# Second block's attentions on one core: a bank for the value products, row halves in turns, earlier compressed turns, squares paired by GpSimd

## The reference, cut to what matters

```python
h = rmsnorm(x, mix_norm[l])
proj = h @ w_in[l]                       # queries, keys, values, gates of both attentions
# sparse attention: 8 heads in 2 groups, head size 64
k_cmp, v_cmp = nsa_compress(...)         # 15 compressed keys/values of the 256 tokens
o_a = nsa_attention(q, k_cmp, v_cmp, k_slc, v_slc, k_win, v_win, gates_a, rel_table)
# linear attention with decay: 4 heads, key size 128, value size 256, chunks of 64 tokens
o_b = gla_attention(q_b, k_b, v_b, log_a)
o_b = rmsnorm(o_b, gla_out_norm)         # over the 256 values of each head: mean of squares
o_b = o_b.reshape(B, S, 1024) * silu(r_b)
y = gm0 * (o_a @ w_branch_nsa) + gm1 * (o_b @ w_branch_gla)
x = x + y @ w_out
```

## Time and profile before

| | |
|---|---|
| median of 3 runs | 2722.19 us |
| lowest, highest | 2721.77, 2728.16 us |
| profiled execution | 2728.3 us, its span 2726.5 us |
| TensorE busy | 2664.9 us, 98% |
| VectorE, ScalarE, GpSimd busy | 1065.1, 1295.2, 1768.0 us (39%, 48%, 65%) |
| mean granted clock of TensorE | 0.991 |

### The profile page before, as it was taken

The page is one execution under the profiler, slowest core; times in us unless marked ns, Lnnn a source line. Parts: engine busy times, 40 slices in busy tenths (PEclk is TensorE's granted clock), DMA queues, the critical chain, the costliest instruction groups (busy, mean ns, idle before and its releaser), DMA issues.

```text
span 2726.5 us, 43454 instructions
## 1 busy us (share of the span) xinstructions
PE 2664.9 (98%) x17423; PEld 2298.5 (84%) x17423; DVE 1065.1 (39%) x2194; ACT 1295.2 (48%) x1851; POOL 1768.0 (65%) x1446
## 2 busy tenths in 40 slices
PE   7999999999999999999999999999999999999998
PEld 5767688778888677988878999999899899989887
DVE  4153564441211545253454322553423414354441
ACT  4445622342222448445545545555545535554553
POOL 2502345334445244868969988559998997757996
PEclk9999999999999999999999999999999999999999
DMA  7564365323223332555635567435555557534554
GB/s 235 147 217 140 124 206 165 109 84 102 93 93 99 68 112 63 155 171 176 205 130 179 191 172 221 125 109 184 187 185 184 186 185 192 171 109 155 185 185 147
DMA packets 397910, 418.81 MB, mean 154 GB/s; under 512 B 80975, under 2 KB 361671, under 8 KB 397492
## 3 DMA queue, kind: packets, MB, share of 16 engines
q1 hardware_dynamic: 397748, 416.52, 49.8%
HBM read 415.42 MB, written 3.16 MB: 154 GB/s over the span
## 4 chain that ended last, share of the span: by engine, by line
PE 91%; DVE 3%; ACT 3%; POOL 1%; issue 1%; DMA 1%; SPq 0%; DVEq 0%; ACTq 0%; POOLq 0%
PE ps L1003 21%; PE ps L987 18%; PE ps L971 14%; PE ps L1655 12%; PE ps L1014 10%; PE ps L1663 6%; PE ps L1031 2%; PE ps L1530 2%; PE ps L1556 2%; POOL ring_r L2066 1%; PE ps L1539 1%; PE ps L1562 1%; ACT arena L2371 1%; PE ps L1786 1%; DMA ring<-in_w_ada 1%
## 5 line engine op out<-in xcount | busy, mean ns | idle before, releaser
L2066 POOL TENSOR_TENSOR ring_r<-ring,ring_hi 128x512 fp32r<-128x512 f32 (+1 forms) x1440 | 1765.5, 1263 | 941.4 <-ACT ring_hi L2120 916.7
L2120 ACT ACTIVATE ring_hi<-ring 128x2048 fp32r<-128x2048 f32 x312 | 596.8, 1914 | 247.0 <-DMA ring<-in_ffn_w_down 104.4
L1003 PE MATMUL ps<-hT_r,ring_hi 128*128 128x256 f32 (+1 forms) x2816 | 467.0, 324 | 5.2 <-issue 2.3
L1003 PEld LDWEIGHTS ps<-hT_r,ring_hi 128*128 128x128 f32 x2816 | 410.1, 191 | 55.3 <-issue 15.1
L1655 PE MATMUL ps<-hT_r,ring_hi 128*128 128x512 f32 x1408 | 340.6, 393 | 0.0
L1655 PEld LDWEIGHTS ps<-hT_r,ring_hi 128*128 128x128 f32 x1408 | 259.6, 189 | 53.5 <-issue 3.3
L987 PE MATMUL ps<-arena_r,ring_hi 128*128 128x256 f32 (+1 forms) x1712 | 291.0, 316 | 1.9 <-DVE arena_r L3429 1.9
L987 PEld LDWEIGHTS ps<-arena_r,ring_hi 128*128 128x128 f32 x1712 | 250.0, 190 | 22.8 <-DVE arena_r L3429 2.3
L1014 PE MATMUL ps<-hT_r,ring_r 128*128 128x256 f32 (+1 forms) x1408 | 237.1, 321 | 0.0
L1014 PEld LDWEIGHTS ps<-hT_r,ring_r 128*128 128x128 f32 x1408 | 207.2, 190 | 19.6
L1663 PEld LDWEIGHTS ps<-hT_r,ring_r 128*128 128x128 f32 x1440 | 184.5, 191 | 6.9
(11 more groups left out here) (401 smaller groups left out, 3363.9 us busy)
## 6 DMA issues: line engine op xcount, KB each, us to landing
ring<-in_w_in SPq DMA_DIRECT2D x74, 1024.0 KB
ring<-in_w SPq DMA_DIRECT2D x64, 1024.0 KB
ring<-in_ffn_w_up SPq DMA_DIRECT2D x44, 1024.0 KB
ring<-in_ffn_w_gate SPq DMA_DIRECT2D x44, 1024.0 KB
ring<-in_ffn_w_down SPq DMA_DIRECT2D x44, 1024.0 KB
ring<-in_w_ada SPq DMA_DIRECT2D x28, 1024.0 KB
arena<-in_w_ada SPq DMA_DIRECT2D x18, 1024.0 KB, 7.8
ring<-in_w_in SPq DMA_DIRECT2D x48, 256.0 KB
```

Of the source, the lines that this page charges most:

```text
L1003: mm = pe.matmul(o, w[0], a[x], start=j == 0 and x == 0, stop=False, skip_group_check=True)
L2066: ins = pool.tensor_tensor(k.ring_lo[s][:, part], k.ring[s][:, part], k.ring_hi[s][:, part], ALU.subtract)
L2120: act.activation(k.ring_hi[s][:, :], k.ring[s][:, :], ACT.Copy).then_inc(k.hi_ready[s], 1)
```

## The change

Five things change, all in the second block's attentions.

1. Bank 7 (`VALUES`) is set aside for the value products of the sparse attention; the others rotate over seven banks meanwhile. TensorE waits before each pair of units until bank 7 has been read.
2. The compressed scores take turns between the row halves product by product, in two banks.
3. The state products of chunks 0 and 1 take turns in the same way, in four banks taken at once; chunk 2 follows.
4. The compressed probabilities are turned in step 1, and the wait for their copy stays in step 2.
5. GpSimd adds the two squares of each head in place (`squares_paired`, four instructions of 128 x 256), in its program before the low part of panel 62 (`PAIRED`). TensorE then waits for `ob_paired` and makes four products with ones instead of eight.

```diff
-    def rotate(self, n):
-        self.bank, self.rotating = 0, n
+    def rotate(self, n, first=0):
+        self.bank, self.rotating = first % n, n
+PAIRED = 62
+VALUES = BANKS - 1
             def sparse_attention(compressed, keys_in):
+                T.rotate(VALUES, T.bank)
                 pe.wait_ge(*k.moved(compressed))
-                for a in range(2):
-                    b = bank()
-                    at = slice(HD * a, HD * a + HD)
-                    for q in range(2):
-                        for c in range(4):
-                            o = (q * 4 + c) * NCMP
+                bs = [bank() for _ in range(2)]
+                for q in range(2):
+                    for c in range(4):
+                        o = (q * 4 + c) * NCMP
+                        for a, b in enumerate(bs):
+                            at = slice(HD * a, HD * a + HD)
                             mm = products(ps[:, b, o:o + NCMP], [(qa[at, c, q * P:q * P + P], kcmp[at, :])])
-                    mm.then_inc(k.bank_done[b], 1)
+                            if (q, c) == (1, 3):
+                                mm.then_inc(k.bank_done[b], 1)
...
-                    if u == 2:
+                    if u == 1:
                         pe.wait_ge(S["cmp_prob"], T.next("cmp_prob"))
...
-                        pe.wait_ge(*k.moved(T.last()))
+                        compressed_turned = T.last()
+                    if u == 2:
+                        pe.wait_ge(*k.moved(compressed_turned))
...
                         if q == 0:
-                            pv = bank()
+                            pv, n = T.again(VALUES)
+                            pe.wait_ge(k.bank_read[pv], n - 1)
...
+                T.rotate(BANKS, T.bank)
             def linear_attention(k_turned):
...
-                for n in range(NCH - 1):
-                    rows = slice(CHUNK * (n % 2), CHUNK * (n % 2) + CHUNK)
-                    for hp in range(2):
-                        b = bank()
-                        for j in range(2):
-                            h = 2 * hp + j
+                for chunks in ((0, 1), (2,)):
+                    bs = {(n, hp): bank() for n in chunks for hp in range(2)}
+                    for h in range(GH):
+                        for n in chunks:
+                            rows, b, j = slice(CHUNK * (n % 2), CHUNK * (n % 2) + CHUNK), bs[n, h // 2], h % 2
...
-                pe.wait_ge(S["ob_squared"], T.next("ob_squared", KD))
+                pe.wait_ge(S["ob_paired"], T.next("ob_paired", GH))
...
-                        mm = products(ps[:, b, j * SEQ:j * SEQ + SEQ], [(ones, sq[:, 2 * h + v, :]) for v in range(2)])
+                        mm = products(ps[:, b, j * SEQ:j * SEQ + SEQ], [(ones, sq[:, 2 * (2 * hp + j), :])])
...
+            def squares_paired():
+
+                sq = area(SQO, KD, SEQ)
+                for h in range(GH):
+                    pool.wait_ge(S["ob_squared"], T.next("ob_squared", 2))
+                    pool.tensor_tensor(sq[:, 2 * h, :], sq[:, 2 * h, :], sq[:, 2 * h + 1, :], ALU.add).then_inc(S["ob_paired"], 1)
+
             for l in range(LAYERS):
                 for j in range(PANELS_2):
+                    if j == PAIRED:
+                        squares_paired()
```

More of the change, by code:

```diff
@@ L365, in __init__ @@
             "cmp_max", "cmp_exp", "cmp_prob", "nsa_max", "nsa_exp", "nsa_prob", "oa_rounded",
-            "oa_split", "rb_ready", "gate0_ready", "ob_squared", "ob_ready", "ob_rounded", "ob_split", "merged_plain",
+            "oa_split", "rb_ready", "gate0_ready", "ob_squared", "ob_paired", "ob_ready", "ob_rounded", "ob_split", "merged_plain",
             "merged_rounded")}
@@ L1959, in linear_attention @@
                 pe.wait_ge(*k.moved(k_turned))
-                for n in range(NCH - 1):
-                    rows = slice(CHUNK * (n % 2), CHUNK * (n % 2) + CHUNK)
-                    for hp in range(2):
-                        b = bank()
-                        for j in range(2):
-                            h = 2 * hp + j
+                for chunks in ((0, 1), (2,)):
[3 more added lines that the diff above has]
+                            rows, b, j = slice(CHUNK * (n % 2), CHUNK * (n % 2) + CHUNK), bs[n, h // 2], h % 2
                             mm = products(ps[:, b, j * DV:j * DV + DV],
                                           [(kst[rows, n // 2, h, :], vb[rows, n // 2, h * DV:h * DV + DV])])
-                        mm.then_inc(k.bank_done[b], 1)
+                            if j == 1:
+                                mm.then_inc(k.bank_done[b], 1)
                 states = T.last()
@@ L2783, in sparse_attention @@
                     if u >= 2 and u % 2 == 0:
-                        attended = skip(1)
+                        attended = T.again(VALUES)
                     if u == HEADS:
@@ L3843, in sparse_attention @@
                     if u >= 2 and u % 2 == 0:
-                        out_of[(u - 2) // 2] = T.take()
+                        out_of[(u - 2) // 2] = T.again(VALUES)
                     if u == HEADS + 1:
```

2 lines of the change are left out of this document (1 added, 1 removed).

## The result

The change makes the kernel slower, by 10.1 us between the medians: 2732.12 us median of six runs (2731.11 to 2733.21) against 2721.98 for the kernel before, six runs beside them; estimated ratio 1.0031, 95% interval 1.0021 to 1.0040. That is 10 us more, where 2.4 us less were forecast and the range ended at 2729. The profiled execution of the changed kernel took 2731.1 us, its span is 2729.3 us. The profiled one of before had already lost 6.6 us when the sparse attention of layer 0 began (1710.35 against 1703.74), so lengths of stretches are compared, not the two spans.

The account below looks back on a forecast made before the run. TensorE, busy 98% of the span, bounds the kernel. Gains of 4.5 and 3.9 us (layers 0, 1) against +3.0 a layer from the pairing give -2.4: 2722.2 to 2719.8 us; 8 in 10 range 2712 to 2729.

Parts of the forecast that it names:

- Compressed scores in turns: Sparse attention's 40 small load and product pairs on TensorE: 3.8 to 2.4 us, 1.4 us less a layer, bounds 0 and 1.4.
- Rival 3: Taking turns does nothing for 15-column products: +2.8 us on the forecast, 2722.6; chance 0.09.
- State products: Twelve 64-row products, 24 loads in 3.54 us: taking turns saves 0.1 us, bounds 0 and 0.25.
- Compressed turns earlier: Turns moved from step 2 to step 1 of the sparse attention: net 0.9 us less a layer.
- Value bank: Two waits a layer for VectorE's copy of the value bank go: 1.3 us less; in layer 1 only, 0.6 more.
- Step 8: Turns waiting for VectorE's four scalings (5.25 us) beside GpSimd's low parts: 0.8 us less, bounds 0 and 0.8.
- Ones products: Squares paired by GpSimd save TensorE four products with ones: 1.6 us less a layer.
- Stand in 62: TensorE stands 2.5 us in panel 62 for its low part, queued on GpSimd behind the adds.
- Its low clock: A 2.5 us stand may bring the low clock: no cost after panel 62, 1.8 us after 66.
- the second stand: TensorE waits 2.1 us before panel 66 for GpSimd's late low part, bounds 0 and 3.1.
- Rival 4: Slower: GpSimd's string from adds to 66 is longer beside VectorE's work, and the low clock comes: 2729.4 us; chance 0.12.
- the shared path: GpSimd's SBUF path is shared with VectorE at two SBUF inputs; GpSimd's instructions then take 2.28 instead of 1.28 us.

Follow-up runs that it names:

- stops after each panel: Changed kernel, but GpSimd waits after each of panels 62 to 67 until its own subtractions of that panel are complete; 2722.46 us (before: 2721.47).
- after 62: Changed kernel, but GpSimd waits once, after panel 62, until its own subtractions of that panel are complete; 2720.34 us (before: 2726.44).
- after the first subtraction: Changed kernel, but GpSimd waits once, inside panel 62, after the first of its four subtractions; 2730.54 us.
- the stop after 63: Changed kernel, but GpSimd waits once, after panel 63, until its own subtractions of that panel are complete; 2717.97 us (before: 2726.44).

## Why the prediction was wrong, point by point

- **Compressed scores in turns:** 1.36 us less a layer (3.86 to 2.50), 1.4 forecast. Rival 3 is out.
- **State products:** the 24 loads in 3.32 instead of 3.54 us: 0.2, near the upper bound, forecast 0.1. (The 1.3 us named beside it isn't half of the serial 4.9 us but 4.9 - 3.54.)
- **Compressed turns earlier:** as read. Step 1's turns (1719.04, 1719.48) are followed by products without a gap, and the wait in step 2 is gone: 0.9.
- **Value bank:** the waits went, 1.3 us. In layer 1 the state products waited for it (below): 0.73 us, forecast 0.6.
- **Step 8:** the four scalings take 3.17 us instead of 5.25 once GpSimd's second panel is moved away. With and without the pairing the way to 62 differs by 0.95 us, 0.8 forecast.
- Together 4.7 and 4.0 us, against 4.5 and 3.9. Layer 1 took 1.5 us less on top, as the low clock after the small products didn't come: the 32 products behind them take 4.10 instead of 5.58 us. I had let that gain cancel against a loss.
- **Ones products:** 1.73 us, forecast 1.6.
- **Stand in 62:** 2.37 us, forecast 2.5.
- **Its low clock:** I wrote that it "would cost nothing", since GpSimd would set when 66 begins. It cost 1.43 us in layer 0 and 1.38 in layer 1 (16 products in 3.51 and 3.46 us), as 66 no longer waited for GpSimd. It wasn't certain to come: with the pairing alone the same 2.37 us stop was followed by 16 products in 2.17 us.
- **The step that failed is the second stand.** The sum had VectorE lose nothing to GpSimd and GpSimd 1 us for each of VectorE's long passes, as in the 13.03 us of the earlier trace rows. That price was taken from strings that were 0.6 us old when VectorE asked. The trace of before had the other case too: the 4.26 us of VectorE's line 3022 at 1402.89, eight us into a string, which the prediction doesn't name. In the string that the change makes, 15.2 us old, VectorE loses 9 us (10.72 against 1.77), GpSimd nothing (20 subtractions in 24.86 us). So the stand came one panel earlier (65, for VectorE's reads of PSUM), was 5.0 us long instead of 2.1, and brought the low clock, 2.4 us. With VectorE let in, the stand before 66 that I forecast is there in some form, against 2.1 and bounds of 0 and 3.1: 2.8 to 3.2 us where no low clock followed the stop in 62 (stops after each panel, after 62, after the first subtraction), 0.2 to 0.6 or none where it did.
- **Rival 4** had the right sign and nearly the size (2729.4) with the wrong mechanism: no more slow instructions of GpSimd, but none, and VectorE slow in their place. It got 0.12, since I looked only for what would make GpSimd later. I had also said "the 2.28 us row agrees" of the shared path, and read it in one direction only.

The row for the wait of layer 1's state products on the value bank, loads in the timeline (before 0.17 us idle, now 0.90):

```profile
2435.82 3.32 PEld L973 LDWEIGHTS ps<-arena 64*128 64x128 f32 x24 [0.90 <-issue]
```

## What to carry to other kernels

Work given to an idle engine is priced by what is queued behind it: here 3.4 us of additions (1.22 + 3 x 0.73) at the right place bring 1.7 us a layer, and two panels earlier they cost some 9 (10.1 us above the kernel before with them, 8.7 below it without, over two layers). When a move turns an in-order engine's loose work into one long string, look at who shares a port with it: take every pass of the other engine that reads or writes SBUF beside that string, and price it both ways, by one instruction and by the whole rest of the string. If the string can't be avoided, one wait of that engine for its own completion (0.1 us), placed less than some 12 us before the other one asks, gave most of it back here: with the stop after 63 the kernel was 8.5 us below the kernel before it ran beside, with none 10 above.

## What the runs showed of the hardware

- A VectorE multiply or copy of 128x1024 in SBUF was kept out for up to 12.8 us beside back-to-back GpSimd subtractions, until 1.08 us (the copy: 0.55) after the last of them. For the first multiply of the outputs this came when GpSimd had run 13.9 us or more without a stop (one exception at 15.4); up to 12.7 us it got in within 2.3 us. Other passes were kept out at 8.0 us (3 of 16) and 10.6 us (1 of 64).
- With a wait of GpSimd for its own completion at most 12.1 us before VectorE asked, the multiply got in within 2.3 us in all nine layers; with the stop 12.7 to 15.4 us before, in two of four.
- While VectorE is kept out GpSimd isn't slowed: 1.24 us from start to start. Where VectorE gets in, the subtraction behind it takes 2.28 us instead of 1.28.
- A stop of TensorE of 2.37 us was followed by a granted clock of 0.54 to 0.60 in some layers and by no low clock in others (16 products in 3.51, or in 2.17 us); each of the stops of 4.2 us and more before panel 65 was followed by it (32 products in 5.6 to 6.8 us instead of 4.0).
- The small products of 64 rows, on the two row halves in turns, start every 0.06 us (40 in 2.50 us); with the compressed ones eight on one half and then eight on the other, the 40 took 3.86.
